# A two-layer decoder trunk on one core: the even output projection split around the group norm with the memory norm between its tiles, cross-attention walked by heads

## The reference, cut to what matters

```
def layer 0:                                     # x is (512, 1024), float32
    p  = rmsnorm(x) @ w_in                       # 2560 columns, one projection
    oa = sliding_window_attention(p[:, :768])    # "SO", 512 wide
    # RWKV-7: r, k, v, decay, a, g = sigmoid(xg) @ g2
    y  = rwkv7_scan(r, decay, k, v, -kk, kk*a)   # state S per head, 8 heads of 64
    y  = groupnorm(y) * lnx_w + lnx_b
    y  = (y + sum(r*k*r_k) * v) * g              # bonus term and output gate
    x  = x + concat(oa, y) @ w_out               # output projection
mk, mv = rmsnorm(mem) @ mem_wk, rmsnorm(mem) @ mem_wv   # 256 memory rows, once
both layers:
    q  = rmsnorm(x) @ xa_wq                      # 4 heads of 128
    x  = x + (softmax(q mk^T / sqrt(128)) mv) @ xa_wo
    x  = x + hierarchical_moe(rmsnorm(x))        # top group of 4, 2 of its 8 experts
```

## Time and profile before

| what | us |
|---|---|
| median of three runs | 2170.55 |
| the profiled execution's own time | 2169.78 |
| its span (first to last instruction) | 2167.6 |
| PE busy | 1985.1 (92%) |
| 206 to 397: the four chunks, PE busy | 170.13 of 191 |
| 397 to 491: group norm and output projection, PE busy | 76.88 of 94 |
| 491 to 514: norm of `XT`, memory rows, PE busy | 15.40 of 23 |
| 571 to 609: softmax of layer 0, PE busy | 25.46 of 38 |
| 1526 to 1564: softmax of layer 1, PE busy | 25.68 of 38 |
| 698 to 1173: experts of layer 0, DMA share | 0.97 |

### The profile page before, as it was taken

The page is one execution under the profiler, slowest core; times in us unless marked ns, Lnnn a source line. Parts: engine busy times, 40 slices in busy tenths (PEclk is TensorE's granted clock), DMA queues, the critical chain, the costliest instruction groups (busy, mean ns, idle before and its releaser), DMA issues.

```text
span 2167.6 us, 21743 instructions
## 1 busy us (share of the span) xinstructions
PE 1985.1 (92%) x8283; PEld 984.0 (45%) x8283; DVE 607.7 (28%) x1018; ACT 453.9 (21%) x755; POOL 162.6 (8%) x201
## 2 busy tenths in 40 slices
PE   7999888698786999999999999989796999999997
PEld 3555888445445333333333443643463333333333
DVE  2154665301214122222222002211223222222123
ACT  2254332202220111111112103421220111111112
POOL 2001443000001000000000000310000000000000
PEclk9999999899995999999999999999887999999999
DMA  5210000206004999999996112103006999999991
GB/s 166 78 39 1 1 1 1 78 20 233 0 3 165 394 426 428 427 426 429 427 428 254 67 40 94 61 0 155 3 22 266 428 427 427 428 426 428 428 415 61
DMA packets 70221, 466.24 MB, mean 215 GB/s; under 512 B 20378, under 2 KB 22538, under 8 KB 45594
## 3 DMA queue, kind: packets, MB, share of 16 engines
q1 hardware_dynamic: 58592, 448.87, 50.4%
q10 hardware_dynamic: 6682, 8.25, 1.1%
q0 software_dynamic: 4896, 8.40, 1.1%
HBM read 468.64 MB, written 6.29 MB: 219 GB/s over the span
## 4 chain that ended last, share of the span: by engine, by line
PE 66%; DMA 23%; DVE 6%; ACT 3%; issue 1%; SPq 0%; POOL 0%; DVEq 0%; ACTq 0%; POOLq 0%
PE ps L942 62%; DMA W<-in_moe_w 23%; PE ps L1110 1%; PE ps L1283 1%; PE ps L1388 1%; DVE XI L1649 1%; PE ps L1361 1%; ACT L661 0%; PE ps L1414 0%; DMA xin<-in_x 0%; SPq L392 0%; DVE HT L1503 0%; DVE xp L1703 0%; DVE small L1693 0%; DVE XJ L1645 0%
## 5 line engine op out<-in xcount | busy, mean ns | idle before, releaser
L942 PE MATMUL ps<-W,xgT 128*64 128x512 f32 x2048 | 455.4, 597 | 10.2 <-DMA W<-in_moe_w 6.2
L942 PE MATMUL ps<-HT,W 128*128 128x512 f32 (+1 forms) x896 | 398.9, 604 | 17.9 <-DVE HT L1503 10.4
L942 PEld LDWEIGHTS ps<-HT,W 128*128 128x128 f32 (+1 forms) x896 | 170.5, 192 | 237.0 <-issue 224.4
L942 PEld LDWEIGHTS ps<-W,xgT 128*64 128x64 f32 x2048 | 144.6, 138 | 293.9 <-issue 277.6
L942 PE MATMUL ps<-W,act 128*64 128x512 f32 x1024 | 232.3, 595 | 2.8 <-ACT ysb L905 2.8
L1863 DVE TENSOR_TENSOR XT<-ps,XT 128x512 f32<-128x512 f32 x240 | 166.0, 692 | 241.7 <-PE ps L942 241.7
L942 PE MATMUL ps<-spread,ysb 128*128 128x512 f32 x512 | 228.3, 599 | 3.2 <-ACT ysb L905 3.2
L942 PEld LDWEIGHTS ps<-spread,ysb 128*128 128x128 f32 x512 | 94.6, 190 | 136.5 <-issue 136.5
L1855 DVE TENSOR_TENSOR act<-ps,sl 128x256 f32<-128x256 f32 x64 | 26.9, 420 | 449.9 <-ACT sl L900 449.9
L942 PEld LDWEIGHTS ps<-W,act 128*64 128x64 f32 x1024 | 70.8, 137 | 136.4 <-issue 136.4
L896 ACT ACTIVATE hs<-ps 128x512 f32<-128x512 f32 x64 | 38.2, 597 | 442.8 <-PE ps L942 442.8
(11 more groups left out here) (356 smaller groups left out, 1805.7 us busy)
## 6 DMA issues: line engine op xcount, KB each, us to landing
W<-in_moe_w SPq DMA_DIRECT2D x192, 2048.0 KB, 17.2
W<-in_od_w_in SPq DMA_DIRECT2D x6, 2048.0 KB, 8.6
W<-in_ev_w_in SPq DMA_DIRECT2D x3, 2048.0 KB, 7.8
W<-in_xa_wq SPq DMA_DIRECT2D x2, 2048.0 KB, 18.6
W<-in_xa_wo SPq DMA_DIRECT2D x2, 2048.0 KB, 7.8
hrows<-hk ACTq DMA_DIRECT2D x8, 512.0 KB, 2.7
W<-in_od_w_out SPq DMA_DIRECT2D x2, 2048.0 KB, 7.7
W<-in_ev_w_in SPq DMA_DIRECT2D x2, 1024.0 KB, 13.6
```

What stands on the lines that cost most here:

```text
L942: return te.matmul(o, l, r, start=first, stop=last)
```

## The change

Five edits, each with its waits:

1. Gate products. The four products of `lora` by `X2` move from behind the last chunk to halves 16, 17, 19 and 20 of the projections (`GATE_AT`), all through bank 3; ACT copies each to a new tile `GG` before the next may be made (`gate_in`).
2. Chunks. The values' turn goes to bank 0 and stands ahead of the key scores; it no longer waits for the state update. That wait stands now before the product of `Sn` by `WT` near the chunk's end, and a new one (`ck_sd`) before the second product of level 1. DVE makes the two factors of the update inside `begin_inverse`. In the last chunk DVE also makes the bonus term, between the levels, and PE its four sums.
3. Output projection. PE makes first eight tiles of four products on `SO` (`half_tile`), added to `XT` by DVE (`add_half`), with the two rounds of head sums among them; then eight tiles of four products on the RWKV half. After the first of these come the turns of the memory rows, after the third the sum of their squares; DVE makes the memory norm ahead of its add of tile 4.
4. `cross` goes by heads: a head's scores, softmax and turn for all 512 tokens; the next heads' queries stand between. In layer 0 the memory values are projected last, in two tiles between the turns. The output projection's first tile waits head by head (`ready`).
5. Loads. `ev_o1` goes to slot 0, `xk` and `xo0` to slot 2, `xq0` to slot 1 and ahead of `xv` (slot 0); the first experts' load stands behind `xv`. The memory rows are issued on ACT's queue after the group norm's root.

```diff
-LOADS = [("ev_kvx", 0), ("ev_q", 2), ("ev_k", 1), ("ev_r", 2), ("ev_v", 0), ("ev_o0", 1), ("ev_o1", 2),
-         ("xk", 0), ("xv", 1), ("xq0", 2), ("xo0", 0),
+LOADS = [("ev_kvx", 0), ("ev_q", 2), ("ev_k", 1), ("ev_r", 2), ("ev_v", 0), ("ev_o0", 1), ("ev_o1", 0),
+         ("xk", 2), ("xq0", 1), ("xv", 0), ("xo0", 2),
...
+GATE_AT = (16, 17, 19, 20)
-TURN_BANK = (0, 2, 3, 1)
+TURN_BANK = (0, 2, 3, 0)
...  PE, projections
+                def gate_tile(j):
+                    if j:
+                        pe.wait_ge(s["gate_in"], j)
+                    mm(ps[:, 3, :], lora[:, 1, j * P:j * P + P], X2[:, 1, :]).then_inc(s["gate_done"], 1)
...  PE, open_chunk
+                    pe.wait_ge(s["ck_vc"], c + 1)
+                    pe.wait_ge(s["ck_tok"], 4 * c + 1)
+                    turn_chunk(c, 3)
                     score_keys(c)
-                    pe.wait_ge(s["ck_vc"], c + 1)
-                    pe.wait_ge(s["ck_sn"], c + 1)
-                    turn_chunk(c, 3)
...  PE, levels
+                            if c and l == 1 and r == 1:
+                                pe.wait_ge(s["ck_sd"], c)
...
+                        if c == NCH - 1 and l <= 4:
+                            pe.wait_ge(s["bonus_p"], l)
+                            if l == 4:
+                                pe.wait_ge(s["bonus_in"], 1)
+                            mm(ps[:, BONUS_BANK[l - 1], :], pair[:, :], KKt[:, l - 1, :]).then_inc(s["bonus_sum"], 1)
...  PE, after the chunks
+                half_tile(0)
                 pe.wait_ge(s["ck_y_in"], NCH + 1)
+                pe.wait_ge(s["bonus_in"], 4)
+                head_sums(lambda j: HT[:, 4 + j, :])
+                half_tile(1)
+                half_tile(2)
+                pe.wait_ge(s["post_a"], 1)
+                head_sums(lambda j: KKt[:, j, :])
+                for mt in range(3, KD):
+                    half_tile(mt)
                 pe.wait_ge(s["post_v"], 2)
+                pe.wait_ge(s["half_in"], KD)
+                residual(... HT[:, k, :]) for k in range(4, KD)], KD, between=memory)
...  PE, cross
+                queries(0)
+                queries(1)
+                scores(0)
+                queries(2)
+                turn(0)
+                scores(1)
+                scores(2)
+                queries(3)
+                turn(1)
+                scores(3)
+                if L == 0:
+                    weights("xv")
+                    memory_values(0)
+                    turn(2)
+                    memory_values(1)
+                    turn(3)
+                    pe.wait_ge(s["proj_taken"], n["proj"])
+                    pv(0)
+                    pv(1)
+                else:
+                    pv(0)
+                    turn(2)
+                    pv(1)
+                    turn(3)
+                pv(2)
+                pv(3)
...  DVE, last chunk
+                        if l == 1 and c + 1 == NCH:
+                            weighted_keys(2)
+                            weighted_keys(3)
+                        if 2 <= l <= 5 and c + 1 == NCH:
+                            bonus(l - 2)
...  DVE, state update
+                        dve.wait_ge(s["ck_s"], c + 1)
+                        ve.tensor_tensor(Sd[:, :, :], ps[:, 1, :]..., Fm[:, :, :], ALU.mult).then_inc(s["ck_sd"], 1)
                         dve.wait_ge(s["ck_sn"], c + 1)
                         st.then(ve.tensor_tensor(Sf, Sf, bcast(fp.unsqueeze(2), [P, 4, P]), ALU.mult))
+                        dve.wait_ge(s["ck_sd"], c + 1)
                         ve.tensor_tensor(Sf, Sf, Sd[:, :, :], ALU.add).then_inc(s["ck_sn"], 1)
```

More of the change, by code:

```diff
@@ L800, in even @@
+                act.wait_ge(s["mem_turned"], 4)
+                for q in range(4):
+                    st.then(sc.activation(memT[:, 2 * q:2 * q + 2, :], ps[:, MEM_BANK[q], :].rearrange("p (k t) -> p k t", k=2), ACT.Copy))
+                norm(memT, memN, MEM)
                 n["xt"] += 8
             def cross(L):
-                if L == 0:
-                    act.wait_ge(s["xt_ready"], n["xt"] - 7)
-                    act.dma_start(memin[:, :, :], a["mem"][0].rearrange("(t p) d -> p t d", p=P)).then_inc(s["mem_in"], 16)
@@ L992, in residual @@
                     for k, (l, r) in enumerate(pairs):
+                        if ready and mt == 0:
+                            ready(k)
                         ins = mm(ps[:, 2 + mt % 2, :], l, r, k == 0, k == len(pairs) - 1)
                     ins.then_inc(s["res_done"], 1)
+                    if between:
+                        between(mt)
                 n["xt"] += 8
@@ new lines, in memory @@
+                def memory(mt):
+                    if mt == 0:
+                        pe.wait_ge(s["mem_in"], 16)
+                        for q in range(4):
+                            for k in (2 * q, 2 * q + 1):
+                                for t in range(MT):
+                                    o = 256 * (k % 2) + t * P
+                                    ins = te.transpose(ps[:, MEM_BANK[q], o:o + P], memin[:, t, k * P:k * P + P], ident[:, :])
+                            ins.then_inc(s["mem_turned"], 1)
+                    if mt == 2:
+                        norm(memN, MEM)
@@ L1245, in cross @@
+                residual(lambda mt: [(W8[slots[mt // 4]][:, k, P * (mt % 4):P * (mt % 4) + P], HT[:, k, :]) for k in range(4, KD)], KD,
+                         between=memory)
             def cross(L):
@@ new lines, in cross, with queries, memory_values, scores @@
+                slot = weights(f"xq{L}")
+                off = 4 * (L + 1)
+                base = n["proj"]
+                def queries(h):
+                    project(bank(), [(W8[slot][:, k, P * h:P * h + P], HT[:, k, :]) for k in range(KD)], first=h == 0)
+                def memory_values(t):
+                    project(bank(), [(memN[:, k, t * P:t * P + P], W8[dict(LOADS)["xv"]][:, k, :]) for k in range(KD)])
+                def scores(h):
+                    pe.wait_ge(s["proj_taken"], base + h + 1)
+                    if h >= 2:
+                        pe.wait_ge(s["sm_exp"], off + h - 1)
+                    for t in range(TT):
+                        ins = mm(ps[:, 4 + 2 * (h % 2) + t // 2, MEM * (t % 2):MEM * (t % 2) + MEM], xq[:, h, t * P:t * P + P], mkT[:, h, :])
+                    ins.then_inc(s["sm_scored"], 1)
```

269 lines of the change are left out of this document (146 added, 123 removed).

## The result

The changed kernel takes 2092.99 us, the median of four runs (2091.24 to 2094.22), against 2169.51 for four runs of before (2167.82 to 2172.23). The ratio is 0.9643, 95% interval 0.9630 to 0.9656. The forecast was 2086, its range 2075 to 2106. The profiled execution has a span of 2089.5 us, 78.1 less than before.

The account below looks back on a forecast made before the run. PE was taken as the bound, with waits and lower clock behind them, ahead of DMA-bound experts. Terms 8.3 - 13.9 - 40.8 - 20.7 - 17.0 = -84.1 took 2169.8 to 2085.7, taken as 2086; range 2075 to 2106.

Parts of the forecast that it names:

- What bounds it: Whole kernel: PE is two thirds of the span; time won before the DMA-bound experts of layer 0 comes through whole.
- Group norm to memory norm: Last chunk to memory keys: half tiles cover the waits, 117.5 us becomes 76.7, gaining 40.8 (bounds 34 to 42).
- Loads: Memory rows, keys, values and experts' weights: issued early enough before use, so the new order costs nothing.
- Cross-attention: Both layers: softmax of a head hidden beside other products, gaining 20.7 us in layer 0 and 17.0 in layer 1.
- Projections: Gate products moved here: 3.5 us of products, waits for ACT's copies and 1.7 for lower clock, sum +8.3.
- Chunks: Four chunks: earlier openings gain 1.6 and 18.6 us, last chunk's keys and sums give some back, sum -13.9.
- my sign: Sign to look for in the new profile: the last chunk's levels 1 to 5 about 6 us longer than its forerunners'.
- The rule weighed: Last chunk's keys beside POOL masks: by the skill's exclusion rule up to 4.4 us instead of 1.0, total 2089.
- (a): Rival, chunk openings: state update stays the bound or POOL's masks come late; chunks -0.7, time 2099; chance 0.13.
- (b): Rival, cross-attention: per-head softmax not covered, every turn waits 2 us, 28 us given back, 2114; chance 0.06.
- (c): Rival, group norm through layer 0 cross-attention: PE's clock falls to 1.2 GHz in the dense stretch, 2264; chance 0.02.
- (d): Rival, output projection's second half: memory turns wait for rows issued too late, at most 2092; chance 0.05.

Follow-up runs that it names:

- experiment 4: The changed kernel with the first gate product moved ahead of block 2's attention turn, so ACT copies it first: 2091.56 us.
- experiment 2: The changed kernel with DVE's small copy of the last decay moved from before level 1 to level 2: 2089.49 us.

## Why the prediction held, and which term did not

- *What bounds it.* Right. Every microsecond won ahead of the experts came through: their stretch still has the DMA engines at 0.98.
- *Group norm to memory norm.* Right to 0.6 us: 76.1 for 76.7. The idle times over 0.7 us are the two that the sum contained, 0.88 and 0.78. Undoing the split gave back its old waits and the slower products behind them, 18.8 us in that stretch.
- *Loads.* Right, they cost nothing: no product there waits for a DMA.
- *Cross-attention.* Right in mechanism, 1.6 and 1.5 us too careful. No turn of layer 0 waits. In layer 1 head 3 is late as laid out, 0.65 and 1.60, but the 0.8 for a slower stretch behind it did not come (3.70 for a product group that takes 3.60 at full clock).
- *Projections.* The wait for ACT's gate copy was 2.46 us (forecast 2.8), and experiment 4 shows that its cause was ACT's order. The 1.7 us for a lower clock did not occur: the product behind it took 1.12.
- *Chunks.* The failed step, and it is a size: -13.9 was -3.5. The update no longer holds PE, as I said, and it ends at 262.1 (my 257.5, and the 5.0 us by which this opening stands later). What I priced too low is what stands beside POOL's masks. I read 1.73 us beside a mask in the earlier trace rows and charged four keys with 1.0 in all; they took 3.0 extra. I did not charge the others at all, since I took their durations from a place where they ran alone; but the edit that lets the key scores go first also moves POOL's masks, so that the state's last add, the small copy and the level's mask (0.9, 1.1 and 1.0 us extra) now fall beside them where chunks 2 to 4 open (in chunk 4 the keys stand in the mask's place). Against the tiny masks the openings of chunks 2 and 3 each show 1.9 of wait from this, and cold products behind it: 1.2 us in chunk 2 (3.41 for 2.21), 1.7 in chunk 3 (3.06 for 2.21 and 2.72 for 1.90). With the masks out of the way the term came to -14.6. The remaining piece is the last chunk: its three sums cost 3.1 for the forecast 2.6, as the first stands in the cold stretch, and a cold level 2 adds 1.6 (3.78 for 2.21). Its levels 1 to 5 are 7.6 us longer than the chunk's before, where my sign had about 6.
- *The rule weighed.* The Trainium skill (SBUF — State Buffer, section "Who interferes with whom") has a VectorE operation with two SBUF inputs and a GpSimd operation that reads SBUF exclude each other; I had worked out up to 4.4 extra for the keys from it, and 2089. The trace bears it out: 3.0 extra is nearer to that than to my 1.0. Asked of every operation of DVE at the openings, not of the keys alone, it would have pointed at the add and the level's mask, which have two such inputs; the small copy has one.
- *Rivals.* (a) comes nearer in the chunks' term, -0.7 for the measured -3.5, and its time of 2099 is 6 us off, where mine is 7. Of its two causes the update's place is refuted, since with nothing of DVE moved the tiny masks gave the gain back, and "POOL's masks come late" names the right engine, but the masks come beside DVE's work, not late for PE. (b) is refuted by turns that wait 0 to 0.65, (c) by clock 1.00 over 176 us, (d) by memory turns at 438.59 right behind a tile.
- *The range.* Its upper side was put together wrongly: the near bounds of my five terms are 6.8 + 8.7 + 8.0 + 8.9 + 2.7 = 35 us from the forecast, not "some 10", and would reach 2121. The measured time lies 7 above the forecast and inside 2075 to 2106. That it is so near is in part luck: one term was 10.4 worse than forecast, and the other four were 1.7, 0.6, 1.6 and 1.5 better, 5.4 in all, which hid half of it.

## What to carry to other kernels

When an edit lets one engine start earlier, lay out anew what runs beside the operations of the others, and charge adds, masks and copies of VectorE that work from SBUF alone beside a GpSimd mask of this size with about one microsecond each; a copy of four columns paid it too. A stall that has to be filled is filled best with work that is there anyway: half tiles on the input that is ready, the next head's queries, another input's norm. And try small repairs together as well as alone, since one repair's gain can depend on another's: moving the copy alone lengthened the held keys behind it. Before adding up gains of a few microseconds, look at how much the same code varies from trace to trace.

## What the runs showed of the hardware

- A copy of 128x4 numbers on DVE took 0.16 us alone and 1.23 beside a POOL mask; between levels, in experiment 2, 0.33. It has one input, so the holding isn't confined to operations with two.
- Operations of DVE that read PSUM for one input are not slowed beside the same masks: 0.41 for `XJ<-ps,XJ` at 264.95, with a POOL mask running from 264.44 on, and 0.42 in the earlier trace rows. Nor was the transposition right behind it (0.71, its usual time), though it works from on-chip memory alone.
- PE's clock after a wait can't be told from the wait's length in these traces: 1.12 us for the product after 2.46 of idle, 2.21 for a level after 2.28, 3.62 after 1.05, in kernels that differ only in small edits. The four chunks, the same code, took 191.1, 193.5 and 197.0 us in three traces, at granted clocks of 0.96, 0.95 and 0.92. A level of the third chunk that waited for nothing took 3.05 (experiment 4), the level before it having waited 2.27 and taken 2.90.
- Starting the chunks earlier, with 2.46 us of idle ahead of them gone, brought 1.4 us alone (2093.0 to 2091.6) and 3.6 where the small copy was moved as well (2089.5 to 2085.9). The two are not clearly apart: the ranges of the runs overlap in both pairs.
